# A two-layer decoder trunk: the residual stream moves from on-chip memory to DRAM

## The chip, the cores and the metric

The kernel runs on one core of a Trainium2 chip. The metric is the device time of one execution, in microseconds (us). A core has five engines that run their own instruction lists and meet through semaphores: TensorE (PE, with its weight loads as PEld), VectorE (DVE), ScalarE (ACT), GpSimd (POOL) and SyncE (SP), which here only issues DMA transfers and waits for them. Compute engines read the on-chip memory, 128 partitions wide; what lies in DRAM has to come through DMA.

## The reference, cut to what matters

`x` is a 1024 x 1024 float32 matrix (4 MB), tokens by channels. Each of two layers reads the whole of it once for the norm and adds one output projection to it. The concatenated output of four mixers (A to D, 512 columns each) is gated and projected back:

```python
def hybrid_layer(x, ...):
    h = rms_norm(x, norm_g)
    proj = h @ w_in
    ...
    y = jnp.concatenate([ya, yb, yc, yd], axis=-1) * jax.nn.silu(gate)
    return x + (y @ w_out)

for l in range(DEPTH):          # DEPTH = 2
    x = hybrid_layer(x, ...)
```

## The kernel before

The residual is one tile `k.x` (the trace calls it `x_res`), 128 partitions by 8 token groups by 1024 channels, 32 KB in each partition. `setup_block` loads it once, and `store_block` writes it once at the very end.

The program is a chain of blocks. At the end of a block all engines meet at a barrier, and nothing of the next block starts before it. After nearly each block stands a small block of its own, `k.clear`, in which POOL sets the used semaphores to zero, one instruction each, and SP issues the load of the first weight chunk of the next projection into the tile `w_next`. A loop (`nc.Fori`) runs over the two layers; in each:

- `norm_block` has ACT square the eight token groups (line 259), turns the sums into 1/rms, and then DVE scales a token group (line 283, `norm_xn`), PE transposes it (line 304), ACT writes its rounded part `h_hi` and DVE the remainder `h_lo`.
- For the mixers A (gla), B (fox), C (mla) and D (lru) come projection blocks (`project_block`), the mixer's own blocks, and an output block `out_block`: four of them a layer, eight in all. What stands behind them is a projection block in six cases, the norm of the second layer in one, and `store_block` in the last.

`out_block` computes `x += y @ w_out[rows of this mixer]` in 16 units of 128 tokens by 512 channels, in the order of `units`. PE takes four units together and makes three passes over them (a product of split operands needs three), so four units are done close together at the end of the third pass. Before the change SP issues one DMA there, the second half of the weights (`w_second`, `gla_wo_raw` in the trace), and DVE adds each unit from PSUM into `x_res`:

```python
for u, (n, t) in enumerate(units):
    dve.wait_ge(unit_done, u + 1)
    at = k.x[:, t, half(n)]
    dve.tensor_tensor(at, at, k.psum[:, u % 8, :], ALU.add).then_inc(added, 1)
```

PSUM holds eight units, so from unit 8 on PE waits for `added` before it reuses a bank.

Of the kernel before, what the change touches and what calls it, by code (L numbers as in the profile page):

```python
# [23 lines left out]
ACT = mybir.ActivationFunctionType  # L24
# [6 lines left out]
P = 128  # L31
BANK = 512
# [28 lines left out]
class Trunk:  # L61


    def __init__(self, nc, dram, out, ctx):
        self.nc, self.dram, self.out, self.ctx = nc, dram, out, ctx
        self.sems, self.used = {}, {}
        self.x = self.sb(ctx, "x_res", [P, TT, D_MODEL])
        self.h_hi = self.sb(ctx, "h_hi", [P, KT, SEQ], F32R)
        self.h_lo = self.sb(ctx, "h_lo", [P, KT, SEQ], F32R)
        self.ident = self.sb(ctx, "ident", [P, P])  # L70
        self.ident_bf = self.sb(ctx, "ident_bf", [P, P], BF16)
        self.mask_bf = self.sb(ctx, "mask_bf", [P, P], BF16)
        self.cos = self.sb(ctx, "cos", [P, TT, ROPE // 2])
        self.sin = self.sb(ctx, "sin", [P, TT, ROPE // 2])
        self.w_next = self.sb(ctx, "w_next", [P, KT * CHUNK_MAX])
        self.w_next_landed = ctx.enter_context(nc.semaphore("w_next_landed"))
        self.plan, self.at = weight_plan(), 0
        self.psum = ctx.enter_context(nc.psum_tensor("psum", [P, 8, BANK], F32))
# [80 lines left out]
def bcast_rows(ap, n):  # L159

    return ap.rearrange("(a m) -> a m", a=1).to_broadcast([n, ap.shape[0]])
# [10 lines left out]
def setup_block(k):  # L172
    nc, d = k.nc, k.dram
    HR = ROPE // 2
    loaded, step, stepped, act_step = (k.sem(n) for n in ("loaded", "dve_chain", "handover", "act_chain"))
    TWO_PI = 2.0 * np.pi
    C1 = float(np.float32(6.28125))
    C2 = 8116.0 / 2 ** 22
    C3 = float(np.float32(TWO_PI - C1 - C2))
    MAGIC = float(1.5 * 2 ** 23)  # L180
    with ExitStack() as s:
        pos_i = k.sb(s, "pos_i", [P, TT], I32)
        pos_f = k.sb(s, "pos_f", [P, TT])
        freq = k.sb(s, "freq", [P, HR])
        ang = k.sb(s, "ang", [P, TT, HR])
        turns = k.sb(s, "turns", [P, TT, HR])
        comp = k.sb(s, "comp", [P, TT, HR])
        low = k.sb(s, "low", [P, TT, HR])
        with nc.Block() as block:
            @block.sync  # L190
            def _(sp):
                sp.dma_start(k.x[:, :, :], d["x"][0].rearrange("(t p) n -> p t n", p=P)).then_inc(loaded, 16)
                sp.dma_start(k.ident[:, :], d["c_ident"]).then_inc(loaded, 16)
                sp.dma_start(k.ident_bf[:, :], d["c_ident_bf"]).then_inc(loaded, 16)
                sp.dma_start(k.mask_bf[:, :], d["c_mask_bf"]).then_inc(loaded, 16)
                sp.dma_start(freq[:, :], d["c_freq"]).then_inc(loaded, 16)
                with nc.allow_non_contiguous_dma(reason="4 KB of positions"):
                    sp.dma_start(pos_i[:, :], d["positions"][0].rearrange("(t p) -> p t", p=P)).then_inc(loaded, 16)
                sp.wait_ge(loaded, 96)

            @block.vector
            def _(dve):
                link = Chain(dve, step)
                dve.wait_ge(loaded, 96)
                link(dve.tensor_copy(pos_f[:, :], pos_i[:, :]))
                link(dve.tensor_tensor(ang[:, :, :], head_bcast(pos_f[:, :], HR),
                                       freq[:, :].unsqueeze(1).to_broadcast([P, TT, HR]), ALU.mult))

                link(dve.tensor_scalar(turns[:, :, :], ang[:, :, :], 1.0 / TWO_PI, MAGIC, ALU.mult, ALU.add))
                link(dve.tensor_scalar(turns[:, :, :], turns[:, :, :], -MAGIC, None, ALU.add))  # L210
                for c in (C1, C2, C3):
                    link(dve.scalar_tensor_tensor(out=ang[:, :, :], in0=turns[:, :, :], scalar=-c, in1=ang[:, :, :],
                                                  op0=ALU.mult, op1=ALU.add))

                link(dve.tensor_scalar(turns[:, :, :], ang[:, :, :], -1.0, None, ALU.mult))
                link(dve.tensor_tensor(comp[:, :, :], turns[:, :, :], ang[:, :, :], ALU.max))

                dve.tensor_scalar(turns[:, :, :], ang[:, :, :], -1.0, float(np.pi), ALU.mult, ALU.add)
                link(dve.tensor_scalar(low[:, :, :], ang[:, :, :], -1.0, -float(np.pi), ALU.mult, ALU.add))
                link(dve.tensor_tensor(ang[:, :, :], ang[:, :, :], turns[:, :, :], ALU.min))  # L220
                link(dve.tensor_tensor(ang[:, :, :], ang[:, :, :], low[:, :, :], ALU.max))
                dve.tensor_scalar(comp[:, :, :], comp[:, :, :], -1.0, float(np.pi / 2), ALU.mult, ALU.add)\
                   .then_inc(stepped, 1)

            @block.scalar
            def _(act):
                act.wait_ge(stepped, 1)
                act.activation(k.sin[:, :, :], ang[:, :, :], ACT.Sin)
                act.activation(k.cos[:, :, :], comp[:, :, :], ACT.Sin).then_inc(act_step, 1)
                act.wait_ge(act_step, 1)  # L230
    k.clear(["loaded", "dve_chain", "handover", "act_chain"])
# [4 lines left out]

def norm_block(k, layer):
    nc, d = k.nc, k.dram
    names = ["loaded", "squares", "mean", "rstd", "act_chain", "normed", "transposed", "hi_done", "lo_done", "dve_chain"]
    loaded, squares, mean, rstd_ready, act_chain, normed, transposed, hi_done, lo_done, dve_chain = map(k.sem, names)  # L240
    with ExitStack() as s:
        gain = k.sb(s, "norm_gain", [P, D_MODEL])
        sq = k.sb(s, "norm_sq", [P, D_MODEL])
        ss = k.sb(s, "norm_ss", [P, TT])
# [3 lines left out]
        with nc.Block() as block:  # L248
            @block.sync
            def _(sp):  # L250
                sp.dma_start(gain[:, :], bcast_rows(d["norm_g"][layer], P)).then_inc(loaded, 16)
                k.fetch(sp, layer, k.plan[0])

            @block.scalar
            def _(act):
                link = Chain(act, act_chain)
                for t in range(TT):

                    link(act.activation(sq[:, :], k.x[:, t, :], ACT.Square, accum_out=ss[:, t:t + 1]))
                act.sem_inc(squares, 1)  # L260
                act.wait_ge(mean, 1)
                link(act.activation(rstd[:, :], ms[:, :], ACT.Ln))
# [10 lines left out]
            def _(dve):  # L273
# [5 lines left out]
                for t in range(TT + 1):  # L279
                    if t < TT:  # L280
                        if t >= 2:
                            dve.wait_ge(transposed, 2 * (t - 1))
                        dve.scalar_tensor_tensor(out=xn[:, t % 2, :], in0=k.x[:, t, :], scalar=rstd[:, t:t + 1],
                                                 in1=gain[:, :], op0=ALU.mult, op1=ALU.mult).then_inc(normed, 1)
                    if t >= 1:
                        for j in range(2):
# [151 lines left out]
def out_block(k, layer, mixer, y, tag):  # L438

    nc = k.nc  # L440
    names = ["w_landed", "w_hi", "w_lo", "y_hi", "y_lo", "unit_done", "added"]
    w_landed, w_hi_ready, w_lo_ready, y_hi_ready, y_lo_ready, unit_done, added = map(k.sem, names)
    NQ = D_MODEL // BANK
    units = [(n, t) for n in range(NQ) for t in range(TT)]
    with ExitStack() as s:
# [3 lines left out]
        w_lo = k.sb(s, tag + "_wo_lo", [P, CT, D_MODEL], F32R)  # L449
        y_hi = k.sb(s, tag + "_y_hi", [P, CT, SEQ], F32R)  # L450
        y_lo = k.sb(s, tag + "_y_lo", [P, CT, SEQ], F32R)

        def half(n):
            return slice(n * BANK, (n + 1) * BANK)

        with nc.Block() as block:
            @block.sync
            def _(sp):
                sp.dma_start(w_second[:, :, :], w_out_rows(k, layer, mixer)[:, :, half(1)]).then_inc(w_landed, 16)

            @block.scalar
            def _(act):
# [13 lines left out]
            def _(dve):  # L476
                for n in range(NQ):
                    dve.wait_ge(y_hi_ready, n + 1)
                    dve.tensor_tensor(y_lo[:, :, half(n)], y[:, :, half(n)], y_hi[:, :, half(n)].bitcast(F32),
                                      ALU.subtract).then_inc(y_lo_ready, 1)  # L480
                for u, (n, t) in enumerate(units):
                    dve.wait_ge(unit_done, u + 1)
                    at = k.x[:, t, half(n)]
                    dve.tensor_tensor(at, at, k.psum[:, u % 8, :], ALU.add).then_inc(added, 1)  # L484

            @block.tensor
            def _(pe):
                for u0 in range(0, len(units), TT // NQ):
                    n, half_tok = units[u0][0], units[u0][1] // (TT // NQ)
                    for i, (a, b) in enumerate(((y_hi, w_hi), (y_lo, w_hi), (y_hi, w_lo))):  # L490
# [7 lines left out]
                        for u in range(u0, u0 + TT // NQ):  # L498
# [5 lines left out]
                                                 start=(c == 0 and i == 0), stop=(c == CT - 1 and i == 2))  # L504
                            if i == 2:
                                last.then_inc(unit_done, 1)
    k.clear(names, fetch_for=layer)


def gate_jobs(sg, mixer, chunks):  # L510
# [1165 lines left out]

def store_block(k):
    with k.nc.Block() as block:  # L1680
        @block.sync
        def _(sp):
            stored = k.sem("stored")
            sp.dma_start(k.out[0].rearrange("(t p) n -> p t n", p=P), k.x[:, :, :]).then_inc(stored, 16)
            sp.wait_ge(stored, 16)


def trunk_kernel(nc, dram, out, parts="ABCD"):
    with ExitStack() as ctx:
        k = Trunk(nc, dram, out, ctx)  # L1690
        setup_block(k)
        with nc.Fori(0, DEPTH) as layer:
# [7 lines left out]
                mla(k, layer)  # L1700
            if "D" in parts:
                lru(k, layer)
        store_block(k)


def constants():
# [39 lines left out]
```

## Time and profile before

| | us |
|---|---|
| median of 3 runs | 3226.34 (3224.7 to 3227.0) |
| profiled execution, first to last instruction (span) | 3222.3 |
| median less span | 4.0 |
| PE busy in the span | 2601.3 (81%) |
| DVE / ACT / POOL busy | 1357.5 / 867.1 / 468.7 |
| moved by DMA | 78.65 MB, mean 24 GB/s |

The profile gives one execution's span alone; the 4.0 us between it and the median of the runs lie before the first and behind the last instruction, and are taken as fixed. The shares of busy time say little about this change, since barriers cut the program into pieces; what counts is which engine each piece waits for, at its start and at its end.

### The profile page before, as it was taken

How to read it: one execution, taken by the hardware profiler on the slowest of the kernel's cores; microseconds unless marked ns; L12 is line 12 of the kernel's file. 1: busy time of each engine (PE TensorE's matmuls, PEld its weight loads, DVE VectorE, ACT ScalarE, POOL GpSimd, SP SyncE). 2: the span in 40 equal slices, each digit the busy share in tenths (PEclk: the TensorE clock that was granted, in tenths of full speed). 3: DMA queues.
4: the chain of work that ended last, by engine and by line, in shares of the span. 5: the costliest groups of instructions: out<-in, count | busy, mean ns of one | idle time of the engine just before them, and what ended most of it. 6: DMA issues, size and time to landing. Idle time of an engine off the chain costs nothing. (4 is left out here: it accounts for less than half of the span.)

```text
span 3222.3 us, 36887 instructions
## 1 busy us (share of the span) xinstructions
PE 2601.3 (81%) x14416; PEld 2124.9 (66%) x14416; DVE 1357.5 (42%) x2296; ACT 867.1 (27%) x1389; POOL 468.7 (15%) x308
## 2 busy tenths in 40 slices
PE   4976678998987898985868776889989878889766
PEld 3855568787766666773657555777877757677545
DVE  3119931522532545515231397225235336364153
ACT  3023310322311424305131233113123124342041
POOL 1115521010020000110111254210100200001111
PEclk9988989999988999998978888889999889999888
DMA  3000010000010000001010000100000100000102
GB/s 114 14 29 1 1 53 15 14 27 27 1 35 25 14 9 14 14 27 30 27 61 14 29 1 3 51 15 14 27 27 2 34 25 14 9 14 14 43 13 79
DMA packets 74534, 78.65 MB, mean 24 GB/s; under 512 B 16080, under 2 KB 63344, under 8 KB 74352
## 3 DMA queue, kind: packets, MB, share of 16 engines
q1 hardware_dynamic: 74352, 76.19, 7.5%
q8 instruction: 118, 1.93, 0.3%
q14 instruction: 64, 0.52, 0.1%
HBM read 71.99 MB, written 4.19 MB: 24 GB/s over the span
## 5 line engine op out<-in xcount | busy, mean ns | idle before, releaser
L892 PE MATMUL psum<-gla_ql,gla_kl 128*128 128x256 f32 x448 | 143.8, 476 | 102.6 <-DVE gla_ql L687 102.5
L892 PEld LDWEIGHTS psum<-gla_ql,gla_kl 128*128 128x128 f32 x448 | 104.4, 243 | 146.5 <-DVE gla_A L759 107.8
L484 DVE TENSOR_TENSOR x_res<-x_res,psum 128x512 f32<-128x512 f32 x128 | 86.0, 685 | 194.0 <-PE psum L503 193.8
L1106 DVE TENSOR_REDUCE fox_nmax<-psum 128x1 f32<-128x128 f32 (+7 forms) x128 | 97.0, 758 | 137.1 <-PE psum L1039 136.4
L1106 DVE TENSOR_REDUCE mla_nmax<-psum 128x1 f32<-128x128 f32 (+7 forms) x128 | 97.0, 758 | 136.6 <-PE psum L1039 135.8
L1125 ACT ACTIVATE mla_q<-psum,mla_nmax 128x128 f32<-128x128 f32 (+7 forms) x128 | 94.8, 741 | 205.6 <-DVE mla_nmax L1106 205.6
L1125 ACT ACTIVATE fox_qa<-psum,fox_nmax 128x128 f32<-128x128 f32 (+7 forms) x128 | 94.8, 741 | 205.6 <-DVE fox_nmax L1106 205.6
L1036 PE MATMUL psum<-fox_kT,fox_qT 66*128 66x512 f32 (+3 forms) x384 | 149.8, 500 | 0.0
L1036 PE MATMUL psum<-mla_kT,mla_qT 96*128 96x512 f32 (+3 forms) x384 | 149.8, 500 | 0.0
L1059 PE MATMUL psum<-fox_v,fox_ka 128*128 128x64 f32 x1152 | 142.7, 270 | 0.0
L1059 PE MATMUL psum<-mla_v,mla_k 128*128 128x64 f32 x1152 | 142.7, 270 | 0.0
L1059 PEld LDWEIGHTS psum<-fox_v,fox_ka 128*128 128x128 f32 x1152 | 138.8, 192 | 0.7 <-DVE fox_ka L1023 0.7
L1059 PEld LDWEIGHTS psum<-mla_v,mla_k 128*128 128x128 f32 x1152 | 138.8, 192 | 0.7 <-DVE mla_k L1023 0.7
L417 PE MATMUL psum<-fox_w_hi,h_hi 128*128 128x256 f32 (+1 forms) x768 | 112.9, 291 | 24.1 <-ACT fox_w_hi L369 24.1
L417 PEld LDWEIGHTS psum<-fox_w_hi,h_hi 128*128 128x128 f32 x768 | 103.2, 198 | 25.5 <-ACT fox_w_hi L369 25.5
L710 POOL TENSOR_TENSOR gla_kl<-gla_kT,gla_E 128x256 f32<-128x256 f32 x112 | 89.1, 802 | 192.7 <-PE psum L892 127.2
L387 POOL TENSOR_TENSOR fox_w_lo<-w_next,fox_w_hi 128x2048 fp32r<-128x2048 f32 x8 | 36.6, 4572 | 542.8 <-ACT fox_w_hi L369 542.8
L417 PE MATMUL psum<-fox_w_lo,h_hi 128*128 128x256 f32 (+1 forms) x768 | 109.7, 286 | 3.4 <-POOL fox_w_lo L387 3.4
L387 POOL TENSOR_TENSOR mla_w_lo<-w_next,mla_w_hi 128x2048 fp32r<-128x2048 f32 x6 | 27.4, 4573 | 579.9 <-ACT mla_w_hi L369 579.9
L417 PE MATMUL psum<-fox_w_hi,h_lo 128*128 128x256 f32 (+1 forms) x768 | 110.5, 287 | 0.0
L759 DVE COPY_PREDICATED gla_A<-gla_masks,psum 128x512 f32<-128x512 int32 x112 | 98.9, 883 | 11.6 <-PE psum L892 6.0
L417 PEld LDWEIGHTS psum<-fox_w_lo,h_hi 128*128 128x128 f32 x768 | 100.1, 192 | 4.6 <-POOL fox_w_lo L387 4.6
(369 smaller groups left out, 5611.9 us busy)
## 6 DMA issues: line engine op xcount, KB each, us to landing
w_next<-in_w_in_dram SPq DMA_DIRECT2D x26, 1024.0 KB, 5.2
w_next<-in_w_out_dram SPq DMA_DIRECT2D x8, 1024.0 KB, 5.1
fox_w_raw<-in_w_in_dram SPq DMA_DIRECT2D x6, 1024.0 KB, 7.2
x_res<-in_x_dram SPq DMA_DIRECT2D x1, 4096.0 KB, 12.6
gla_w_raw<-in_w_in_dram SPq DMA_DIRECT2D x4, 1024.0 KB, 6.9
out_dram<-x_res SPq DMA_DIRECT2D x1, 4096.0 KB, 11.7
gla_w_raw<-in_w_in_dram SPq DMA_DIRECT2D x2, 1088.0 KB, 5.2
fox_w_raw<-in_w_in_dram SPq DMA_DIRECT2D x2, 1056.0 KB, 9.6
```

The source lines that it names most:

```text
L387: pool.tensor_tensor(lo[:, j % ring, :, :width], chunk(j), hi[:, j % ring, :, :width].bitcast(F32), ALU.subtract).then_inc(w_lo_ready, 1)
L417: last = pe.matmul(o, lhsT, rhs, start=(kk == 0 and n == 0), stop=(kk == KT - 1 and n == 2))
L484: dve.tensor_tensor(at, at, k.psum[:, u % 8, :], ALU.add).then_inc(added, 1)
L710: pool.tensor_tensor(kl[:, m % RING, :, :], kT[:, :, tok(c)], E[:, c % 2, j - 1, :, :], ALU.mult)\
L759: dve.copy_predicated(later(A[:, c % 2, :, :], B), m, ps).then_inc(masked, 1)
L892: last = pe.matmul(k.psum[:, n % NB, g * HH * HALF:(g + 1) * HH * HALF], kl[:, m % RING, g, :], ql[:, m % RING, g, :, :] .rearrange("p h t ...
L1036: pe.matmul(out[:, c0:c1], qT[:, h, qt * P:(qt + 1) * P], kT[:, h, c0:c1], start=True, stop=(c1 < n))
L1059: last = pe.matmul(k.psum[:, B_O + qt % 2, h * HEAD:(h + 1) * HEAD], pt_sb[:, u % 2, b * P:(b + 1) * P], v[:, b, h * HEAD:(h + 1) * HEAD], ...
L1106: dve.tensor_reduce(nmax[:, u:u + 1], score_ap(u), AX_X, ALU.max, negate=True)\
L1125: act.activation(p_sb[:, u % 2, :n], score_ap(u), ACT.Exp, bias=nmax[:, u:u + 1], accum_out=rsum[:, u:u + 1]).then_inc(probs, 1)
```

## The change

The tile `k.x` is gone. The output tensor in DRAM holds the residual from the start: `setup_block` copies `x` from one DRAM tensor to the other. `norm_block` loads the whole residual from it into a tile of its own, `norm_x`, and the squares wait for that load. `out_block` brings each unit on chip through six buffers (`xt`), adds, and writes it back. `store_block` is gone. The names that `out_block` clears go from 7 to 19, those of the norm from 10 to 11.

```diff
-        self.x = self.sb(ctx, "x_res", [P, TT, D_MODEL])
...
-                sp.dma_start(k.x[:, :, :], d["x"][0].rearrange("(t p) n -> p t n", p=P)).then_inc(loaded, 16)
+                sp.dma_start(k.out[0].rearrange("(t p) n -> p t n", p=P), d["x"][0].rearrange("(t p) n -> p t n", p=P)).then_inc(loaded, 16)
...
+        x = k.sb(s, "norm_x", [P, TT, D_MODEL])
...
+                sp.dma_start(x[:, :, :], k.out[0].rearrange("(t p) n -> p t n", p=P)).then_inc(x_landed, 16)
                 sp.dma_start(gain[:, :], bcast_rows(d["norm_g"][layer], P)).then_inc(loaded, 16)
                 k.fetch(sp, layer, k.plan[0])
...
+                act.wait_ge(x_landed, 16)
                 for t in range(TT):
 
-                    link(act.activation(sq[:, :], k.x[:, t, :], ACT.Square, accum_out=ss[:, t:t + 1]))
+                    link(act.activation(sq[:, :], x[:, t, :], ACT.Square, accum_out=ss[:, t:t + 1]))
...
+    XR = 6
+    x_names = [f"x_{what}{i}" for what in ("in", "stored") for i in range(XR)]
+    x_in, x_stored = [k.sem(n) for n in x_names[:XR]], [k.sem(n) for n in x_names[XR:]]
...
                 sp.dma_start(w_second[:, :, :], w_out_rows(k, layer, mixer)[:, :, half(1)]).then_inc(w_landed, 16)
+
+                def rows(u):
+                    n, t = units[u]
+                    return k.out[0, t * P:(t + 1) * P, half(n)]
+
+                for i in range(len(units) + 3):
+                    if i < len(units):
+                        if i >= XR:
+                            sp.wait_ge(x_stored[i % XR], 16 * (i // XR))
+                        sp.dma_start(xt[:, i % XR, :], rows(i)).then_inc(x_in[i % XR], 16)
+                    if i >= 3:
+                        u = i - 3
+                        sp.wait_ge(added, u + 1)
+                        sp.dma_start(rows(u), xt[:, u % XR, :]).then_inc(x_stored[u % XR], 16)
+                for i in range(XR):
+                    sp.wait_ge(x_stored[i], 16 * len(range(i, len(units), XR)))
...
                 for u, (n, t) in enumerate(units):
+                    dve.wait_ge(x_in[u % XR], 16 * (u // XR + 1))
                     dve.wait_ge(unit_done, u + 1)
-                    at = k.x[:, t, half(n)]
+                    at = xt[:, u % XR, :]
                     dve.tensor_tensor(at, at, k.psum[:, u % 8, :], ALU.add).then_inc(added, 1)
...
-    k.clear(names, fetch_for=layer)
+    k.clear(names + x_names, fetch_for=layer)
...
-        store_block(k)
```

SP's list at the start of a layer. Before, it holds the gain vector and the first weight chunk:

```order
L1692 UNCONDITIONAL_BRANCH [waits barrier_Pool_Activation_PE_DVE_SP_release]
L249 UNCONDITIONAL_BRANCH
L251 ISA
L251 DMA norm_gain<-in_norm_g_dram 128x1024
L99 ISA
L99 DMA w_next<-in_w_in_dram 128x8x256
```

Now:

```order
L1708 UNCONDITIONAL_BRANCH [waits barrier_Pool_Activation_PE_DVE_SP_release]
L251 UNCONDITIONAL_BRANCH
L253 DMA norm_x<-out_dram 128x8x1024
L254 ISA
L254 DMA norm_gain<-in_norm_g_dram 128x1024
L98 ISA
L98 DMA w_next<-in_w_in_dram 128x8x256
```

The 4 MB load stands ahead of the two that were there. SP's list at the last four units of the first output block (gla) and behind it. Before, SP goes straight from the weight load to the barrier and then to the next fetch:

```order
L459 DMA gla_wo_raw<-in_w_out_dram 128x4x512
L456 UNCONDITIONAL_BRANCH
L120 UNCONDITIONAL_BRANCH [waits barrier_Pool_Activation_PE_DVE_SP_release]
L123 ISA
L99 ISA
L99 DMA w_next<-in_w_in_dram 128x8x256
```

Now, from the load of unit 14 on (`x` with a number repeats the row; a row lists only the waits that are still open at that place):

```order
L477 DMA gla_xt<-out_dram 128x512 [waits x_stored2]
L481 DMA out_dram<-gla_xt 128x512 [waits added]
L477 DMA gla_xt<-out_dram 128x512 [waits x_stored3]
L481 DMA out_dram<-gla_xt 128x512 [waits added] x4
L464 UNCONDITIONAL_BRANCH [waits x_stored3,x_stored4,x_stored2,x_stored5,x_stored1,x_stored0]
L119 UNCONDITIONAL_BRANCH [waits barrier_Pool_Activation_PE_DVE_SP_release]
L122 ISA
L98 ISA
L98 DMA w_next<-in_w_in_dram 128x8x256
```

A load and a store for each unit now stand between the weight load and the barrier, and the last stores have to be complete before it. On the DVE list each add of the gla block gets a second wait:

```order
L503 TENSOR_TENSOR gla_y_lo<-gla_gate,gla_y_hi 128x4x512 [waits y_hi] x2
L509 TENSOR_TENSOR gla_xt<-gla_xt,psum 128x512 [waits unit_done,x_in0]
L509 TENSOR_TENSOR gla_xt<-gla_xt,psum 128x512 [waits unit_done,x_in1]
L509 TENSOR_TENSOR gla_xt<-gla_xt,psum 128x512 [waits unit_done,x_in2]
L509 TENSOR_TENSOR gla_xt<-gla_xt,psum 128x512 [waits unit_done,x_in3]
```

There are 16 such adds in a block, in the same order as before.

## Rows read from the trace of the kernel before

**Rows 1.** The page: busy time of PE, and the granted clock in 40 slices

```profile
PE 2601.3 (81%) x14416; PEld 2124.9 (66%) x14416; DVE 1357.5 (42%) x2296; ACT 867.1 (27%) x1389; POOL 468.7 (15%) x308
...
PEclk9988989999988999998978888889999889999888
```

**Rows 2.** Timeline 0 to 75 us: start, duration, engine, line, operation

```profile
0.74 0.45 SPq L192 DMA_DIRECT2D x_res<-in_x_dram  x1
...
3.92 1.34 SPq L198 DMA_DIRECT2D pos_i<-in_positions_dram  x1
14.75 0.17 DVE L205 CAST pos_f<-pos_i 128x8 f32<-128x8 int32 x1 [14.75 <-DMA pos_i<-in_positions_dram]
...
20.21 1.28 ACT L259 ACT_TABLE_LOAD   x1 [1.02 <-PEq L114]
...
21.50 1.06 ACT L259 ACTIVATE norm_sq<-x_res 128x1024 f32<-128x1024 f32 x1
```

**Rows 3.** DMA issues: tile, count, KB of each, median us from issue to landing

```profile
w_next<-in_w_in_dram SPq DMA_DIRECT2D x26, 1024.0 KB, 5.2
...
x_res<-in_x_dram SPq DMA_DIRECT2D x1, 4096.0 KB, 12.6
...
out_dram<-x_res SPq DMA_DIRECT2D x1, 4096.0 KB, 11.7
...
mla_w_uq<-in_mla_w_uq_dram SPq DMA_DIRECT2D x4, 384.0 KB, 3.3
...
mla_w_ukv<-in_mla_w_ukv_dram SPq DMA_DIRECT2D x4, 256.0 KB, 3.5
...
lru_w_r<-in_lru_w_r_dram SPq DMA_DIRECT2D x4, 64.0 KB, 2.4
```

**Rows 4.** Timeline around the end of layer 0 and the second norm

```profile
1611.10 0.69 DVE L484 TENSOR_TENSOR x_res<-x_res,psum 128x512 f32<-128x512 f32 x1 [0.22 <-PE psum L503]
1615.99 1.28 ACT L259 ACT_TABLE_LOAD   x1 [46.82 <-issue]
1616.43 0.35 SPq L251 DMA_DIRECT2D norm_gain<-in_norm_g_dram  x1
...
1617.29 1.06 ACT L259 ACTIVATE norm_sq<-x_res 128x1024 f32<-128x1024 f32 x1
```

**Rows 5.** Timeline in the two norms: PE's transposes of one token group

```profile
42.39 1.09 PE L304 MATMUL psum<-ident,norm_xn 128*128 128x128 f32 x8 [1.30 <-DVE norm_xn L283]
...
1638.18 1.97 PE L304 MATMUL psum<-ident,norm_xn 128*128 128x128 f32 x8 [0.42 <-DVE norm_xn L283]
```

**Rows 6.** Timeline in and behind the first output block (gla), then fox

```profile
429.92 2.47 DVE L484 TENSOR_TENSOR x_res<-x_res,psum 128x512 f32<-128x512 f32 x4
...
441.40 0.69 DVE L484 TENSOR_TENSOR x_res<-x_res,psum 128x512 f32<-128x512 f32 x1 [0.22 <-PE psum L503]
...
464.07 0.69 DVE L484 TENSOR_TENSOR x_res<-x_res,psum 128x512 f32<-128x512 f32 x1 [0.22 <-PE psum L503]
465.25 0.39 SPq L99 DMA_DIRECT2D w_next<-in_w_in_dram  x1
466.17 1.20 SPq L350 DMA_DIRECT2D fox_w_raw<-in_w_in_dram  x2
470.45 1.91 ACT L369 ACTIVATE fox_w_hi<-w_next 128x2048 fp32r<-128x2048 f32 x1 [45.85 <-DMA w_next<-in_w_in_dram]
```

**Rows 7.** Timeline: last add of the kernel and the final store

```profile
3208.37 0.69 DVE L484 TENSOR_TENSOR x_res<-x_res,psum 128x512 f32<-128x512 f32 x1 [0.22 <-PE psum L503]
3210.22 0.40 SPq L1684 DMA_DIRECT2D out_dram<-x_res  x1
```

**Rows 8.** Timeline at the end of gla's mixing block, which clears 24 names

```profile
411.69 0.75 DVE L778 SCALAR_TENSOR_TENSOR gla_gate<-psum,gla_g_out,gla_gate 128x512 f32<-128x512 f32 x1 [1.21 <-PE psum L928]
414.69 1.91 ACT L465 ACTIVATE gla_wo_hi<-w_next 128x2048 fp32r<-128x2048 f32 x1 [4.94 <-PEq L114]
```

**Rows 9.** Windows: length, busy PE, PEld, DVE, ACT, POOL; granted clock, DMA share, GB/s

```profile
957.00:967.00 10.00, 9.15 (x51) 8.85 (x51) 0.49 (x2) 1.17 (x1) 7.08 (x2) 0.61 0.01 2
```

More of the change, by code:

```diff
@@ L238, in norm_block @@
     nc, d = k.nc, k.dram
-    names = ["loaded", "squares", "mean", "rstd", "act_chain", "normed", "transposed", "hi_done", "lo_done", "dve_chain"]
-    loaded, squares, mean, rstd_ready, act_chain, normed, transposed, hi_done, lo_done, dve_chain = map(k.sem, names)
+    names = ["loaded", "x_landed", "squares", "mean", "rstd", "act_chain", "normed", "transposed", "hi_done", "lo_done",
+             "dve_chain"]
+    (loaded, x_landed, squares, mean, rstd_ready, act_chain, normed, transposed, hi_done, lo_done,
+     dve_chain) = map(k.sem, names)
     with ExitStack() as s:
+        x = k.sb(s, "norm_x", [P, TT, D_MODEL])
         gain = k.sb(s, "norm_gain", [P, D_MODEL])
@@ L282, in _ @@
                             dve.wait_ge(transposed, 2 * (t - 1))
-                        dve.scalar_tensor_tensor(out=xn[:, t % 2, :], in0=k.x[:, t, :], scalar=rstd[:, t:t + 1],
+                        dve.scalar_tensor_tensor(out=xn[:, t % 2, :], in0=x[:, t, :], scalar=rstd[:, t:t + 1],
                                                  in1=gain[:, :], op0=ALU.mult, op1=ALU.mult).then_inc(normed, 1)
@@ L451, in out_block @@
         y_lo = k.sb(s, tag + "_y_lo", [P, CT, SEQ], F32R)
+        xt = k.sb(s, tag + "_xt", [P, XR, BANK])
         def half(n):
@@ L1673, in lru_mix @@
     project_block(k, layer, gate_jobs(sg, 3, (1,)), "lru_gate1", side=Side([], lambda act: None, gated))
[L1679 to L1685, printed above, removed]
 def trunk_kernel(nc, dram, out, parts="ABCD"):
```

## The prediction

> **What bounds the kernel now.** I read the page first. PE is busy 81% of the span [rows 1], but this change touches no matmul, so the share says only that PE's own work stays. The program is a chain of blocks with barriers, so I went to the timeline at the places where the residual is loaded, read and stored, and asked at each what ends last. Four such places exist.
>
> At the start the last thing that DVE waits for is the landing of `pos_i`, a 4 KB transfer issued at 3.92 and landed at 14.75: it stands in SP's queue behind the 4 MB of `x`, which takes 12.6 us from its issue at 0.74, to 13.3 [rows 2, 3]. The transfer of `x` sets the end of the setup.
>
> In the norm nothing is waited for at the start: ACT's first square starts at 21.50, as soon as its table is in [rows 2]. In layer 1 it is the same, at 1617.29 [rows 4].
>
> In an output block PE sets the pace. The adds come in fours, 10.9 us apart: from unit 6 at 441.40 to unit 15, two groups and one unit (0.91) on, it is 22.67, so a group is 10.88 [rows 6]. DVE waits for PE there and the residual is never waited for.
>
> Behind an output block the last add ends at 464.76, SP issues the next weight chunk 0.49 us later, and ACT starts on it when it has landed, at 470.45 [rows 6]. Everything in this stretch is in series. At the very end the same add ends at 3209.06, the final store is issued at 3210.22, takes 11.7 us, and the span ends at 3222.3 [rows 3, 7]: a tail of 13.2 us.
>
> **The change part by part.**
>
> *Setup.* The 4 MB go from DRAM to DRAM. The trace has no such transfer. It has the two halves of it: a load of 12.6 us and a store of 11.7 us, each of 4 MB [rows 3]. If reading and writing overlap fully the copy takes 12.6 (no change); if they share one limit in full it takes their sum, 24.3 (+11.7). Less than nothing is excluded, since the same 4 MB must be read. Between the two I take 19.0, a little above the middle (18.4), because both sides now use the same memory: **+6.4**. All of it is on the path, `pos_i` being queued behind. The page "DMA: Bandwidth & Descriptors" of the Trainium skill (Latency and other measured facts) lists 207 GB/s for copies between HBM tensors whose row pitch does no harm; as an estimate from that figure, 4.19 MB would take 20.3 us, and this term would be +7.7 rather than +6.4. No run here shows it yet.
>
> *The two norms.* SP's first instruction there is now the 4 MB load. In layer 0 the block opens at about 20.2 (ACT's table load starts at 20.21), so `x` lands at 20.2 + 12.6 = 32.8, where the first square stood at 21.50: +11.3. In layer 1 the block opens at 1615.99 and SP gets to its first DMA about 0.2 later: 1616.2 + 12.6 = 1628.8 instead of 1617.29: +11.5 [rows 2 to 4]. Together **+22.8**; with the store's 11.7 as lower price +21.0. The gain (512 KB) and the first weight chunk (1 MB) now queue behind 4 MB, but they are wanted 12 and 35 us after the squares begin, and at the 5.2 us that 1 MB takes they are early by more than 5 us [rows 3]. No work covers the load: the block before is over, and everything in the norm needs `x`. PE idles 11 us longer and may run its transposes at half clock, but in the norm it waits for DVE at either level (8 transposes in 1.09 us with 1.30 idle before, or in 1.97 with 0.42) [rows 5], so that costs nothing.
>
> *Inside the output blocks.* 16 loads and 16 stores of 256 KB a block. The first four loads stand behind the weight half and are wanted when the first adds come, 15 us into the block. Later ones: load 6 is the tightest. It waits until unit 0 is stored in full. Unit 0 is added by 430.6, the store lands about 2.9 later, the load 2.9 after that, and 0.5 for issues: 436.9, against unit 6 at 441.40 [rows 6]. There are 4.5 us of slack, and nobody waits: **0**. The cover is the 10.9 us that PE needs for four units; if it were gone, two landings a group would be open. The added wait on DVE stands in front of a wait for PE that ends later, so it costs nothing either, and DVE's adds are on no path but the last one.
>
> *Behind the output blocks.* SP now waits for the last stores before the barrier. The store of unit 15 is issued when its add ends (say 0.1), and its landing is the price. A store of 256 KB is in no row. Near it: 64 KB in 2.4, 384 KB in 3.3, 256 KB in 3.5 (queued behind the 384 KB), 1 MB in 5.2 [rows 3]. The line through 384 KB and 1 MB has 0.3 us for each 100 KB, so 256 KB takes 2.9; bounds 2.4 and 3.5. That the direction matters little is read from the 4 MB pair, 11.7 out and 12.6 in [rows 3]. So +3.0 at each of the seven boundaries inside the kernel: **+21.0** (17.5 to 25.2). The next fetch, the barrier and PE are all behind it. The page "DMA: Bandwidth & Descriptors" (Anatomy of one DMA) speaks against cheap stores: completion waits for the last byte's confirmation, which "can cause a surprisingly long delay especially when the write target is HBM"; its fit would give an estimate of 2.6 us for 256 KB, or 18.9 for the seven. The trace so far does not bear out the long delay, 11.7 being the shorter of the pair.
>
> *Twelve more names to clear.* Clearing 7 names and passing the two barriers takes 1.16 (3209.06 to 3210.22) [rows 7]; with 24 names it takes 2.25 (412.44 to 414.69) [rows 8]. That is 0.064 a name, 0.8 for twelve. In six boundaries the 5.2 us landing of `w_next`, issued first, hides it [rows 6]; without that cover it would be 4.6. At the loop's end it counts: **+0.8**. The norm's one more name is 0.06 each time, left out.
>
> *The end.* The tail of 13.2 becomes 0.1 + 2.9 (last store) + 1.2 (barriers, clear) + 0.8 (twelve names) + 0.4 (what lay behind the landing, 3210.22 + 11.7 to 3222.3) = 5.4: **-7.8** [rows 3, 7].
>
> *Clock.* Gaps of PE get longer by 3 us behind output blocks. They already cost: after one, 10 us of projection ran at a granted clock of 0.61, most of it at 1.2 GHz instead of 2.4 [rows 9]. The shift moves such stretches by an unknown little. From the norm's start to the last add layer 0 took 1590.9 us and layer 1 1592.4 [rows 2, 4, 7], the same work; so I count 0, and 3 either way.
>
> Sum: 6.4 + 22.8 + 0 + 21.0 + 0.8 - 7.8 = **+43.2** on a span of 3222.3, 3265.5. With the 4.0 us outside the span, 3269.5 for the median, 1.3% above 3226.3.
>
> **The rivals.**
>
> *Long completions (0.17).* DRAM writes confirm late, or the copy runs at the sum of both halves. With the copy at 24.3 us (+5.3) and the eight last stores at 4.5 us each (8 x 1.6 = 12.8) the time is 3288. For it: the memory is on both sides of the copy. Against it: the 4 MB store.
>
> *The six buffers run dry (0.06).* Two landings in series must fit into 10.9 us less issue times; from 5.2 us a landing on DVE is late, PE finds its bank not yet added and waits. At 6.5 us that is 2 x 1.3 for each of three groups in eight blocks, +62, and +29 from the eight last stores: about 3360. Against it: the row of 1 MB has 5.2 and the units are a quarter of that.
>
> *The DMAs cost less than their parts (0.10).* Copy at 12.6 (-6.4), loads at 11.7 (-1.8), stores at 2.4 (-4.0): 3257. A smaller cost inside this range is the same mechanism as the forecast.
>
> *The clock gives it back (0.02).* TensorE's half-clock stretches open the projections behind each output block: 10 us at 0.61 means 7.8 us at 1.2 GHz, so 3.9 us lost [rows 9]. If the shifted starts fell where full clock is granted at once, six boundaries and two norms gave back at most 8 x 3.9 = 31, which does not pay for 43; only with the cheap DMAs above (+31) does it reach 3226. It would be no slower from there on. Against it: gaps grow, and low clock follows a gap.
>
> *Forecast (0.65)*: the sum with its terms within their bounds, 3259 to 3282.
>
> **How the numbers follow.** The likeliest is 3269.5. Low end: the cheap DMAs with a clock gain of 1, 3256. High end: 3287, just under the long completions' 3288, which leaves half of them, the dry buffers and the clock outside, under 0.2. A run of this kernel scatters by about 0.04% and two kernels can be told apart from 0.2%, 6.5 us. Slower by more than that: 0.97; within it 0.02; faster 0.01.
>
> **What the new profile would show.** DVE's first work at about 21 instead of 14.75 (setup). In both norms ACT's first square waits for `norm_x`, about 12.6 us after SP's first DMA. Adds in fours still 10.9 us apart, no wait for `x_in` beyond the first group. From the last add of a block to the fetch of `w_next` 3.5 instead of 0.49. A tail of 5.4. Wrong it would be if a 256 KB store takes over 4 us, if the copy takes over 24, or if DVE's adds wait for the loads.

## The result and the profile after

The changed kernel takes 3266.6 us in the median of 4 runs (3263.0 to 3270.5), against 3225.5 for the kernel before (3224.3 to 3227.0, 4 runs): a ratio of 1.0128, 95% interval 1.0113 to 1.0142. It is slower by 41 us. The profiled execution took 3263.0 and has a span of 3261.2, 38.9 above the span of before.

First the page of the changed kernel. PE's busy time is the same within 0.2% (2606.4 against 2601.3), and DMA moves 150.0 MB where it was 78.7; the shares say nothing more.

```profile
span 3261.2 us, 37390 instructions
...
PE 2606.4 (80%) x14416; PEld 2129.8 (65%) x14416; DVE 1358.4 (42%) x2296; ACT 866.5 (27%) x1389; POOL 468.9 (14%) x308
...
DMA packets 112444, 150.02 MB, mean 46 GB/s; under 512 B 20192, under 2 KB 67456, under 8 KB 112256
```

The timeline of its first 64 us answers to [rows 2]:

```profile
0.73 0.75 SPq L191 DMA_DIRECT2D out_dram<-in_x_dram  x1
...
16.75 0.17 DVE L204 CAST pos_f<-pos_i 128x8 f32<-128x8 int32 x1 [16.75 <-DMA pos_i<-in_positions_dram]
...
22.21 1.28 ACT L263 ACT_TABLE_LOAD   x1 [1.02 <-PEq L113]
22.27 0.38 SPq L253 DMA_DIRECT2D norm_x<-out_dram  x1
...
35.30 1.06 ACT L263 ACTIVATE norm_sq<-norm_x 128x1024 f32<-128x1024 f32 x1 [11.81 <-DMA norm_x<-out_dram]
```

DVE starts 2.0 later than before, so the copy cost 2.0 (it took 14.4 us where the load of `x` took 12.6). The norm opens at 22.21 and its first square starts 13.1 later; it was 1.3. ACT's row names the load as what ended the wait. The same in layer 1, beside [rows 4]:

```profile
1634.52 0.69 DVE L509 TENSOR_TENSOR lru_xt<-lru_xt,psum 128x512 f32<-128x512 f32 x1 [0.22 <-PE psum L528]
1642.68 1.28 ACT L263 ACT_TABLE_LOAD   x1 [50.21 <-issue]
1642.97 0.39 SPq L253 DMA_DIRECT2D norm_x<-out_dram  x1
...
1656.91 1.06 ACT L263 ACTIVATE norm_sq<-norm_x 128x1024 f32<-128x1024 f32 x1 [12.95 <-DMA norm_x<-out_dram]
```

From the last add's end (1635.21) to the next block is 7.47 instead of 4.20, and the square waits 14.2 behind the block's opening instead of 1.3. In and behind the first output block, beside [rows 6], DVE, SP and ACT of the changed kernel:

```profile
443.11 2.47 DVE L509 TENSOR_TENSOR gla_xt<-gla_xt,psum 128x512 f32<-128x512 f32 x4
...
454.65 0.69 DVE L509 TENSOR_TENSOR gla_xt<-gla_xt,psum 128x512 f32<-128x512 f32 x1 [0.22 <-PE psum L528]
...
477.32 0.69 DVE L509 TENSOR_TENSOR gla_xt<-gla_xt,psum 128x512 f32<-128x512 f32 x1 [0.22 <-PE psum L528]
480.88 0.41 SPq L98 DMA_DIRECT2D w_next<-in_w_in_dram  x1
482.40 1.03 SPq L354 DMA_DIRECT2D fox_w_raw<-in_w_in_dram  x2
486.08 1.91 ACT L373 ACTIVATE fox_w_hi<-w_next 128x2048 fp32r<-128x2048 f32 x1 [49.27 <-DMA w_next<-in_w_in_dram]
```

The adds still wait for PE and for nothing else, and from unit 6 to unit 15 it is 22.67 us, to the hundredth what it was. Only behind the last add the rows differ: 2.87 us to the fetch instead of 0.49. The transfers, by tile, count, KB and median us to landing, beside [rows 3]; the last row is from the window 478 to 481 us alone, where the last store of that block lands:

```profile
norm_x<-out_dram SPq DMA_DIRECT2D x2, 4096.0 KB, 13.5
...
gla_xt<-out_dram SPq DMA_DIRECT2D x32, 256.0 KB, 5.2
out_dram<-gla_xt SPq DMA_DIRECT2D x32, 256.0 KB, 3.2
...
out_dram<-in_x_dram SPq DMA_DIRECT2D x1, 4096.0 KB, 14.4
...
out_dram<-gla_xt SPq DMA_DIRECT2D x1, 256.0 KB, 2.0
```

And the last add of the kernel, beside [rows 7]: it ends at 3256.45, and the span at 3261.2.

```profile
3255.76 0.69 DVE L509 TENSOR_TENSOR lru_xt<-lru_xt,psum 128x512 f32<-128x512 f32 x1 [0.22 <-PE psum L528]
```

The same marks read in both timelines (first DVE work, opening of a norm, first square, weight load, first and last add of each output block, next work of SP and ACT) split the 38.9 us, up to rounding. A *stage* here runs from ACT's first work behind an output block to the first add of the next one; six stand behind a gla, fox or mla output block, and gla's own two run from the first square of a norm to gla's first add:

| where | predicted | measured |
|---|---|---|
| setup, until DVE starts | +6.4 | +2.0 |
| the two norm loads | +22.8 | +24.7 (11.8 and 12.9) |
| last add to the next fetch, six output blocks | +18.0 | +14.3 (2.38 each) |
| loop's end, with twelve names more to clear | +3.8 | +3.3 |
| tail behind the last add, 13.2 to 4.8 | -7.8 | -8.5 |
| inside the eight output blocks, and `w_next` landings | 0 | +0.7 and +0.2 |
| the six stages from there to the next output block | 0 | +4.8 |
| gla's stages from the first square on, two | 0 | -2.7 |
| sum | +43.2 | +38.9 |

### The profile page after: what moved, and what is told of

Its sections match the earlier page's. It is cut to its first block and busy times, and to the rows that moved or that the text cites. A ratio compares the mean times of both kernels' runs of the same rounds, so it can differ in the third digit from the quotient of the medians.

```text
span 3261.2 us, 37390 instructions
## 1 busy us (share of the span) xinstructions
PE 2606.4 (80%) x14416; PEld 2129.8 (65%) x14416; DVE 1358.4 (42%) x2296; ACT 866.5 (27%) x1389; POOL 468.9 (14%) x308
## 5 line engine op out<-in xcount | busy, mean ns | idle before, releaser
L308 PE MATMUL psum<-ident,norm_xn 128*128 128x128 f32 x128 | 27.7, 392 | 94.9 <-DVE norm_xn L287 94.9
## 6 DMA issues: line engine op xcount, KB each, us to landing
norm_x<-out_dram SPq DMA_DIRECT2D x2, 4096.0 KB, 13.5
```

Source lines behind the costliest of these rows:

```text
L308: last = pe.transpose(k.psum[:, u % 8, c * P:(c + 1) * P], xn[:, t % 2, kk * P:(kk + 1) * P], k.ident[:, :])
```

## The experiments

Spans and rows are of one profiled execution each; times in us are medians. The kernel before ran beside each, and its own median moved between these series (3225.5 beside the changed kernel, 3223.9 beside the first four, 3225.05 beside the next three, 3224.8 beside the last two). A difference of two medians from different series is uncertain by that much, and is given against the kernel beside it where it matters.

**Twelve more names to clear, alone.** The kernel before with

```diff
+    extra = [f"extra{i}" for i in range(12)]
...
-    k.clear(names, fetch_for=layer)
+    k.clear(names + extra, fetch_for=layer)
```

> The kernel before, with twelve unused semaphores more to clear behind each output block and nothing else of the change. Theory A (the added clears count only where no fetch covers them): +0.9 us at the loop's end and +0.9 in the tail, nothing at the six other boundaries, 1.8 in all. Rival B (the clears also delay the second weight chunk of the next projection, and PE feels that): the six stages behind a gla, fox or mla output block get 0.6 to 1.0 longer each as well, 6 in all.

Measured: 3225.65 against 3223.92, ratio 1.0008 (0.9999 to 1.0018); 1.7 us, as theory A has it, though the interval still holds zero. The loop's end grew by 1.2 (4.20 to 5.40). The next projection's second weight load is indeed issued 1.52 behind the first instead of 0.97 (here behind the mla block):

```profile
1397.93 0.37 SPq L99 DMA_DIRECT2D w_next<-in_w_in_dram  x1
1399.45 0.37 SPq L350 DMA_DIRECT2D lru_w_raw<-in_w_in_dram  x1
```

But the six stages, from ACT's first work to the next output block's first add, are 443.4, 406.5, 175.0, 440.1, 406.5 and 174.6 against 443.1, 406.8, 175.0, 443.5, 406.7 and 174.6: none is longer by more than 0.3, and one is 3.4 shorter, which nothing in the edit explains. So the late second chunk costs nothing, and rival B falls; what made those stages longer in the changed kernel (444.0, 407.9, 175.5, 443.9, 407.7, 175.6) is something else.

**The norm's load in eight parts.** The changed kernel with

```diff
-                sp.dma_start(x[:, :, :], k.out[0].rearrange("(t p) n -> p t n", p=P)).then_inc(x_landed, 16)
+                for t in range(TT):
+                    sp.dma_start(x[:, t, :], k.out[0, t * P:(t + 1) * P, :]).then_inc(x_group[t], 16)
...
-                act.wait_ge(x_landed, 16)
                 for t in range(TT):
+                    act.wait_ge(x_group[t], 16)
```

> The changed kernel with the norm's 4 MB load cut into eight loads of 512 KB, each with its own semaphore, so that the square of a token group waits for its own group only. Theory A (the load is simply in series with the squares): only the last square stays behind the last landing, the norm's start to the end of the squares shrinks from 22.5 us to about 14.5, 8 us a norm, 16 below the changed kernel in all. Rival B (512 KB transfers run slower than one of 4 MB, at some 2 us each): no gain or 3 to 4 us a norm.

Measured: 3250.2, 16.4 below the changed kernel; ratio to before 1.0081 (1.0064 to 1.0098). Against the kernel before beside each it is +26.2 where the changed kernel was +41.1, 14.9 less. Its timeline shows the first square and the first work behind the last one:

```profile
22.19 1.28 ACT L266 ACT_TABLE_LOAD   x1 [1.02 <-PEq L113]
...
25.93 1.06 ACT L266 ACTIVATE norm_sq<-norm_x 128x1024 f32<-128x1024 f32 x1 [2.46 <-DMA norm_x<-out_dram]
...
36.39 0.17 DVE L283 TENSOR_SCALAR norm_ms<-norm_ss 128x8 f32<-128x8 f32 x1 [15.76 <-ACTq L267]
```

From the block's opening to `norm_ms` it is 14.2 us; in the changed kernel it was 22.6. In layer 1 the same stretch went from 23.7 to 15.5. Theory A had forecast 14.5: the load and the squares were in series. The span fell by 12.5 and not by these 16.6, because the work of gla behind `norm_ms`, which the edit does not touch, took 2.6 and 1.3 us longer in this trace. Such scatter comes back below.

**The wait for the last stores, later.** The changed kernel, with the buffers in a lasting tile and, for gla, fox and mla,

```diff
# out_block, SP:
-                for i in range(XR):
-                    sp.wait_ge(x_stored[i], 16 * len(range(i, len(units), XR)))
# next project_block, SP, behind its weight loads:
+                for i in range(len(k.pending) // 2):
+                    sp.wait_ge(k.sems[f"x_stored{i}"], 16 * len(range(i, 16, 6)))
```

> The changed kernel, but the wait for the last stores of the gla, fox and mla output blocks stands at the end of SP's list in the next projection block (the six buffers live in a tile that stays allocated, and their semaphores are cleared behind that block). Behind the lru block the wait stays. Theory A (each of the six waits is 2.4 us of pure series): last add to next fetch is 0.5 again, 14 us below the changed kernel. Rival B (the stores still in flight slow the fetch that is now issued beside them): the fetch lands up to 2 us later, 2 to 8 us below.

Measured: 3247.0, 19.6 below the changed kernel; ratio to before 1.0069 (1.0052 to 1.0086). Against the kernel before beside each it is +23.1 where the changed kernel was +41.1, 18.0 less.

```profile
479.77 0.69 DVE L515 TENSOR_TENSOR xt<-xt,psum 128x512 f32<-128x512 f32 x1 [0.22 <-PE psum L534]
481.43 0.41 SPq L100 DMA_DIRECT2D w_next<-in_w_in_dram  x1
482.36 1.74 SPq L356 DMA_DIRECT2D fox_w_raw<-in_w_in_dram  x2
486.79 1.91 ACT L377 ACTIVATE fox_w_hi<-w_next 128x2048 fp32r<-128x2048 f32 x1 [47.56 <-DMA w_next<-in_w_in_dram]
```

From the end of the add (480.46) to the fetch it is 0.97, not 0.49, since the last store still has to be issued; six times 1.9 is 11.4. The fetch lands as before (5.36 to ACT, it was 5.20), so rival B falls. The gain in the median is larger than theory A's 14. The trace, taken of the slowest of the four executions, is 14.2 shorter than that of the changed kernel, and its parts are these: the borders give 11.1 up to ACT's first work, the six stages behind them another 8.2 (442.5, 406.2, 174.4, 442.4, 406.3, 174.6), and gla's two stages, in front of which no late wait stands, take back 2.3 and 2.9, the loop's end 0.6; the rest is under 1. So the wait itself is shown at 1.9 a border. Why the stages behind got shorter too is looked into under "The last landing, alone".

**Four buffers instead of six.**

```diff
-    XR = 6
+    XR = 4
```

> The changed kernel with four buffers instead of six. Theory A (two landings in series must fit between groups; with four buffers the load of unit i waits for the store of unit i-4, and the store of unit i-3 is issued behind that load, so SP does one store landing of 3.2 us and one issue per unit): 3.7 us a unit against PE's 2.7, the adds come evenly instead of in fours, a block takes 15 to 24 us longer, 120 to 190 in all. Rival B (the turnaround is hidden in any case): within 3 us of the changed kernel.

Measured: one run of 3359.9, span 3358.0, 97 above the changed kernel's. DVE and SP in its gla block:

```profile
459.08 0.69 DVE L509 TENSOR_TENSOR gla_xt<-gla_xt,psum 128x512 f32<-128x512 f32 x1 [3.02 <-DMA gla_xt<-out_dram]
459.69 0.33 SPq L477 DMA_DIRECT2D gla_xt<-out_dram  x1
460.06 0.43 SPq L481 DMA_DIRECT2D out_dram<-gla_xt  x1
462.83 0.69 DVE L509 TENSOR_TENSOR gla_xt<-gla_xt,psum 128x512 f32<-128x512 f32 x1 [3.07 <-DMA gla_xt<-out_dram]
```

The adds come one by one, 3.75 us apart, and each waits for its load. The mechanism is theory A's; the size was 12 to 14 us a block and not 15 to 24. From the start of the first add to the end of the last it is 47.0 to 48.6 us where it was 34.8 to 35.5. That is one run, but its distance is far beyond any scatter seen here. Six buffers are thus free here because of their number, not because 256 KB transfers are quick.

**The last landing, alone.** The kernel before, with this behind the weight load of each output block:

```diff
+                n, t = units[-1]
+                sp.wait_ge(added, len(units))
+                sp.dma_start(k.out[0, t * P:(t + 1) * P, half(n)], k.x[:, t, half(n)]).then_inc(k.sem("tail"), 16)
+                sp.wait_ge(k.sem("tail"), 16)
```

> The kernel before, where SP in each output block waits for the last add, stores that one unit (256 KB) to DRAM and waits for it before the barrier; nothing else of the change, the whole store at the end stays. Theory A (behind an output block the changed kernel pays for the last landing and for a longer gap of PE, and the 31 other transfers of a block are free): +2.4 us from the last add to SP's next work at the seven boundaries and +2.4 in the tail, gap of PE 10.0 instead of 7.6, the granted clock in the first 10 us behind it as in the changed kernel and those six stages 0.4 to 1.0 longer each; adds in a block as before; 19 to 25 in all. Rival B (the clock or the streaming costs inside the blocks): 10 or less.

Measured: 3250.0 against 3225.05, 25 us, ratio 1.0077 (1.0060 to 1.0094). One wait behind each block gives all that the changed kernel shows behind its blocks: 2.70 from the last add to the fetch (0.49 before), a gap of 9.9 instead of 7.6, and stages of 444.8, 407.6, 176.4, 444.2, 407.9 and 176.2, 7.3 longer in sum than before. "Gap" is from here on the time from the last add's end to PE's next work; PE's own idle time is 0.7 to 0.8 us longer. The stages grew by 0.7 to 1.7 each, more than the 0.4 to 1.0 expected. The store itself:

```profile
out_dram<-x_res SPq DMA_DIRECT2D x8, 256.0 KB, 2.1
```

Where a stage begins to differ is read from windows of 5 us each, from PE's first matmul behind layer 0's fox output block on (columns as in [rows 9]; the granted clock is the third number from the end). Kernel before, gap 7.7:

```profile
956.60:961.60 5.00, 4.14 (x17) 3.84 (x18) 0.00 (x0) 1.27 (x1) 4.96 (x2) 0.50 0.00 0
961.60:966.60 5.00, 5.00 (x31) 5.00 (x31) 0.42 (x1) 0.00 (x0) 2.48 (x1) 0.68 0.01 3
```

Changed kernel, gap 10.0:

```profile
975.50:980.50 5.00, 4.13 (x17) 3.84 (x18) 0.00 (x0) 1.27 (x1) 4.96 (x2) 0.50 0.00 0
980.50:985.50 5.00, 5.00 (x27) 5.00 (x27) 0.42 (x1) 0.00 (x0) 2.47 (x1) 0.56 0.01 3
```

This experiment, gap 10.0:

```profile
966.90:971.90 5.00, 4.15 (x17) 3.85 (x18) 0.00 (x0) 1.27 (x1) 4.98 (x2) 0.50 0.00 0
971.90:976.90 5.00, 5.00 (x28) 5.00 (x28) 0.42 (x1) 0.00 (x0) 2.44 (x1) 0.58 0.01 3
```

The late wait, gap 8.3:

```profile
972.90:977.90 5.00, 4.10 (x18) 3.81 (x19) 0.00 (x0) 1.27 (x1) 4.94 (x2) 0.57 0.00 0
977.90:982.90 5.00, 5.00 (x45) 5.00 (x44) 0.85 (x2) 0.00 (x0) 2.54 (x1) 1.00 0.01 3
```

The same matmuls stand there in all four. In the second window 31, 27, 28 and 45 of them get done, with a granted clock of 0.68, 0.56, 0.58 and 1.00. As the clock has two levels, 1.2 and 2.4 GHz, a mean of 0.68 means that 3.2 of the 5 us were at the lower one. So PE was back at 2.4 GHz 8.2 us after its first matmul in the kernel before, after 9.4 and 9.2 behind the gaps of 10 us, and after 4.3 behind the one of 8.3. The stage that begins here differs in the same order: against the kernel before it is 1.0 and 0.8 longer, and 0.6 shorter. At 52 us into it the distances are +0.5, +0.4 and -0.7, so only about half of what the longer ones lose can come from the clock at its start; the rest builds up later in the stage and was not traced to a cause. That the length of the stages goes with the gap is shown; the whole way from the gap to the time is not. A stage can gain from a slightly longer gap: the effect has no fixed sign in the gap's length.

**Why the norm's load takes 13 to 14 us.** Two kernels, one execution each (3264.8 and 3262.0). In one SP waits for the load before it issues the gain and the first weight chunk:

```diff
                 sp.dma_start(x[:, :, :], k.out[0].rearrange("(t p) n -> p t n", p=P)).then_inc(x_landed, 16)
+                sp.wait_ge(x_landed, 16)
```

> The changed kernel, but SP issues the gain and the first weight chunk of the norm only when the 4 MB have landed. Asks why that load takes 13.0 us in layer 0 and 13.9 in layer 1, where 4 MB of x took 12.6 before. Theory A (the two transfers issued behind it take a share): 12.6 or less in both norms. Rival B (it is the place it reads from, or the time since it was written): 13.0 and 13.9 again.

In the other the norm reads the input tensor:

```diff
-                sp.dma_start(x[:, :, :], k.out[0].rearrange("(t p) n -> p t n", p=P)).then_inc(x_landed, 16)
+                sp.dma_start(x[:, :, :], d["x"][0].rearrange("(t p) n -> p t n", p=P)).then_inc(x_landed, 16)
```

> The changed kernel, but both norms load from the input tensor instead of the output tensor; so the second layer normalises x of layer 0 and its output is not the reference's. Theory B (layer 1's load is slower because of what it reads, written shortly before by 128 stores of 256 KB): 13.0 in both layers. Rival A (it is not the source): 13.0 and 13.9 again.

The DMA rows of the first and of the second, medians over the two norms (13.5 in the changed kernel):

```profile
norm_x<-out_dram SPq DMA_DIRECT2D x2, 4096.0 KB, 13.4
```

```profile
norm_x<-in_x_dram SPq DMA_DIRECT2D x2, 4096.0 KB, 13.6
```

From its issue to the first square, the load takes 12.9 in layer 0 and 14.0 in layer 1 in the first run, 13.3 and 13.9 in the second, 13.0 and 13.9 in the changed kernel. Neither the neighbours in the queue nor the source make layer 1's load a microsecond longer. (Of the 128 stores of 256 KB that the second expectation names, 64 stand before that load.) In layer 1, and not in layer 0, the DMA view of these 14 us in the changed kernel also lists instruction loads beside it:

```profile
DMA packets 1372, 4.95 MB, mean 353 GB/s; under 512 B 30, under 2 KB 219, under 8 KB 1367
...
q14 instruction: 4, 0.03, 1.2%
q8 instruction: 1, 0.02, 0.4%
```

They are 0.05 of 4.95 MB. That they are the cause was not tried. It stays open, at 1 us.

**The residual on chip, with the series taken away.** The kernel before, where x is loaded behind the small loads in eight parts that only the squares wait for, and the lru output blocks store each unit when it is added:

```diff
# setup_block, SP, behind the small loads:
+                for t in range(TT):
+                    sp.dma_start(k.x[:, t, :], d["x"][0, t * P:(t + 1) * P, :]).then_inc(k.sem(f"x_group{t}"), 16)
+                sp.sem_inc(k.sem("stored"), 256)
# norm_block: ACT waits for x_group[t]; SP waits for "stored" >= 256 behind its loads; "stored" is cleared
# out_block, SP, lru only:
+                    for u, (n, t) in enumerate(units):
+                        sp.wait_ge(added, u + 1)
+                        sp.dma_start(k.out[0, t * P:(t + 1) * P, half(n)], k.x[:, t, half(n)]).then_inc(k.sem("stored"), 16)
# store_block: only waits for "stored" >= 256
```

> The residual on chip as before, with what the runs so far showed to be series taken away: setup issues its small loads first and the 4 MB of x behind them in eight parts that only the squares wait for, and each lru output block stores its units to DRAM as they are added, so that nothing is left to store at the end. Theory (these were pure series): the setup ends at about 10 us instead of 20, the squares of layer 0 end at about 20.5 instead of 31, -10 to -12; tail 4.5 to 5 instead of 13.2, -8; 18 to 20 faster than before, 0.6%. Rival (the x load is late enough to hold the squares, or the clock takes it back): -8 to -12.

Measured: 3204.7 against 3224.8 (5 and 15 runs), ratio 0.9936 (0.9923 to 0.9950), 20 us faster than the kernel before. Its timeline:

```profile
11.84 1.06 ACT L262 ACTIVATE norm_sq<-x_res 128x1024 f32<-128x1024 f32 x1
...
21.32 0.17 DVE L279 TENSOR_SCALAR norm_ms<-norm_ss 128x8 f32<-128x8 f32 x1 [12.34 <-ACTq L263]
...
3198.49 0.69 DVE L491 TENSOR_TENSOR x_res<-x_res,psum 128x512 f32<-128x512 f32 x1 [0.22 <-PE psum L510]
```

`norm_ms` starts at 21.3 where it was 31.0, and the span ends at 3201.6, 2.4 behind the last add, where it was 13.2. The squares follow each other without a gap. The tail gave 3 more than expected. In layer 0 the lru output block took 1.4 more than before and the loop's end 1.0 more, which was not looked into.

**The residual in DRAM, with all of it.** The changed kernel with the late wait, the eight norm loads, and the copy behind the small loads in eight parts, each norm load waiting for its own part:

```diff
# setup_block, SP, behind the small loads:
+                for t in range(TT):
+                    sp.dma_start(k.out[0, t * P:(t + 1) * P, :], d["x"][0, t * P:(t + 1) * P, :]).then_inc(k.sem(f"copied{t}"), 16)
# norm_block, SP:
+                for t in range(TT):
+                    sp.wait_ge(k.sem(f"copied{t}"), 16)
+                    sp.dma_start(x[:, t, :], k.out[0, t * P:(t + 1) * P, :]).then_inc(x_group[t], 16)
```

> The residual in DRAM as in the changed kernel, with the late wait of e3 and the norm's eight loads of e2, and in the setup the copy goes behind the small loads in eight parts, each norm load waiting for its own part. Theory: e2's gain (16.5 together with e3's 19.6 makes 3266.6 - 36 = 3230.5) and some 12 from the setup, which ends at 10 instead of 22 while the copy runs into the norm: 3216 to 3224, level with the kernel before. Rival (copy and norm load share one limit): the copy and load of 8 MB end no earlier than 5 + 27 us, 3226 to 3232.

Measured: 3226.2 against 3224.8, ratio 1.0009 (1.0000 to 1.0018): level with the kernel before, 40 us below the changed one. The setup did not give its 12 us:

```profile
10.42 1.28 ACT L270 ACT_TABLE_LOAD   x1 [1.02 <-PEq L115]
...
20.64 1.06 ACT L270 ACTIVATE norm_sq<-norm_x 128x1024 f32<-128x1024 f32 x1 [8.93 <-DMA norm_x<-out_dram]
...
31.04 0.17 DVE L287 TENSOR_SCALAR norm_ms<-norm_ss 128x8 f32<-128x8 f32 x1 [22.18 <-ACTq L271]
```

The block opens at 10.4, but the first part is on chip only at 20.6, behind the copy, and `norm_ms` comes at 31.0, 5.3 before the eight-part load without this (36.4). Copy and load of 8 MB in one queue ended about where the rival put them (32), and the time lies in the rival's 3226 to 3232, not in the theory's 3216 to 3224.

That does not make the residual in DRAM free. The kernel before had transfers in series too, and the run on chip without them took 3204.7 beside the same kernel before, 21.5 us less than this one. Of the 20.0 us between the two traces 17 lie at the norms (`norm_ms` comes 9.7 later in layer 0, and 7.3 more pass from the end of layer 0's last add to it in layer 1).

## Why the prediction was right, step by step

The time lies 2.9 us under the forecast of 3269.5, and the mechanism is the one forecast: the residual's transfers cost where nothing stands beside them, at the block borders, and nothing inside the output blocks. The terms were off in both directions.

- *What bounds the places*, and with it the sign: right. No output block changed by more than 0.2 us.
- *Setup, +6.4*: mis-sized, +2.0. The copy of 4 MB took 14.4 us against 12.6 for the load. I had put it above the middle between overlap (12.6) and series (24.3) because both sides use the same memory; it lies near full overlap. The 207 GB/s of the Trainium skill ("DMA: Bandwidth & Descriptors", Latency and other measured facts), which that page gives for tiles of 16 KiB per partition at a row pitch of 512 KiB, would have been worse still, at an estimated 20.3. This copy, with rows of 4 KB, moved 4.19 MB in 14.4 us, 291 GB/s.
- *Norm loads, +22.8*: +24.7. Layer 1's load took 13.9 us, 1 more than layer 0's; that one is open. That they are pure series with the squares is shown by the eight-part load, which gave 8.4 us a norm back in layer 0 and 16.4 in all.
- *Inside the blocks, 0*: right, +0.7 over eight blocks. But a load took 5.2 in the median and not 2.9, and a store 3.2, so the slack at unit 6 was smaller than the 4.5 us I gave: in the first gla block its load landed 2.2 us before its add, and that of unit 7 1.9 before, which was the tightest. That 4 buffers cost 97 us shows how near the edge is. The rival of dry buffers was priced by landing time; what decides is the number of buffers, through the store that must land before the load behind it on SP's list is issued.
- *Behind the blocks, +21.0*: mis-sized, +16.7 for seven at 2.38. The landing of a last store is 2.0 us, not 2.9: the line through 384 KB and 1 MB did not hold at 256 KB, and even the lower bound of 2.4 (64 KB) was too high. The warning in the Trainium skill ("DMA: Bandwidth & Descriptors", Anatomy of one DMA) of a long delay for writes to HBM does not show here, at 2.0 us for 256 KB. Its fit is one for transfers issued by GpSimd, and these are issued by SP; the estimate of 2.6 from it was nearer than mine and still above the trace.
- *Names to clear, +0.8*: right, 0.9 at the loop's end (3.27 less 2.38), 1.2 in the run with the clears alone; under the fetch nothing, as forecast.
- *Tail, -7.8*: -8.5, the same 0.9 of the landing.
- *Clock, 0 and 3 either way*: missed for the stages behind output blocks. The six got 4.8 us longer; the run with one wait alone shows the same with no streaming at all (7.3), so it is the longer gap and not the traffic. Two gla stages got 2.7 shorter in the same trace, but those scatter without any cause in the change: in the two runs that only add clears or a wait they were 0.8 and 3.8 us longer in layer 0, and 0.9 and 2.2 shorter in layer 1. That the two together stay within 3 is luck. The stretch of [rows 9] was also too large a price for all borders: behind three of the six, the kernel before was back at 2.4 GHz after 4.3 to 4.5 us, behind the other three after 8.0 to 8.3.
- *The 4.0 us outside the span*: wrong. The profiled run of the changed kernel took 3263.0 with a span of 3261.2, 1.8 around it. Most of the 4.0 was the distance of the profiled run from the median. That is why spans differ by 38.9 and medians by 41.1.

The errors of the terms, -4.4, +1.9, -4.3, -0.7 and +4.8 among them, cancelled for a part; the closeness of the total is more luck than its terms earn. The clock as the way back to an even time was rightly held small: against the kernel before it never gave more than 4 us over the six stages.

## What to carry to other kernels

Moving data from on-chip memory to DRAM costs little where a queue runs beside a busy engine, and its full latency at each barrier or loop that must see it complete. So count the places where a transfer stands alone, and at each the time of that transfer: here 67 MB inside eight blocks cost 0.7 us, seven last stores of 256 KB cost 16.7, and two loads of 4 MB cost 24.7. A wait for stores at the end of a block could stand one block later, and a whole-tensor load ahead of a loop over its parts could be cut into those parts. Tried one by one, these two edits gave back 18 and 15 of the 41 us, each against the kernel before beside it; together with the setup's copy cut up as well they gave back 40. Before deepening or thinning a ring, write out which landing each issue waits for on its queue: one landing per unit in series decides, and between four and six buffers lay 97 us. And before an edit's price is read from one trace, look at stages that the edit does not touch: here they moved by up to 3.8 us.

## What the runs showed that I had not expected

- A copy of 4 MB from DRAM to DRAM took 14.4 us, hardly more than a load (12.6) or a store (11.7) of the same size.
- A store of 256 KB into a quiet queue landed after 2.0 to 2.1 us; amid the ring's other transfers after 3.2.
- The gap before PE's next work goes with the length of what follows, and not in one direction. In sum the six stages took 2049.7 us behind gaps of 7.6 to 7.8 us in the kernel before and in the streamed one on chip (2046.1 with the clears alone, by the one stage named there), 2046.4 and 2045.8 behind 8.1 to 8.5 us (late wait, and the last DRAM version), and 2052.0 to 2057.0 behind 9.9 to 10.6 us (the changed kernel at 2054.6, and the four runs with its borders or one wait alone).
- The way back to the loop's start costs 4.2 us between the last add and the next block (1.2 from the last add to the final store, outside the loop); no engine is busy in it.
